# Two norms of a fused transformer pair: sums of squares taken behind each tile, the factor formed per token, the last division and the output split

## The reference, cut to what matters

```python
def rmsnorm_2(x, g):
    xf = x.astype(jnp.float32)
    y = xf * lax.rsqrt(jnp.mean(xf * xf, axis=-1, keepdims=True) + EPS)
    return (y * g.astype(jnp.float32)).astype(x.dtype)
...
        x = x + merged @ w_out[l]
        hn = rmsnorm_2(x, ffn_norm_g[l])
        gu = hn @ w_up[l]                     # 1024 -> 2 x 2816
        h = jax.nn.silu(gu[..., :FFN_HIDDEN]) * gu[..., FFN_HIDDEN:]
        x = x + h @ w_down[l]                 # 2816 -> 1024
    return rmsnorm_2(x, final_norm_g)
```

## Time and profile before

| what | value |
|---|---|
| time, median of 3 runs | 1966.1 us (1965.91 to 1969.23) |
| the profiled execution's own time | 1966.58 us |
| its span, first to last instruction | 1964.8 us |
| PE busy | 1749.0 us, 89% of the span |
| DVE / ACT / POOL busy | 441.5 / 282.9 / 116.6 us |
| chain that ended last | PE 76%, DMA 15%, SPq 3%, DVE 3%, ACT 2%, issue 1% |

### The profile page before, as it was taken

How to read it: one execution, slowest core, us unless ns; L and a number is a source line. 1 busy time by engine, 2 the same in 40 slices (tenths; PEclk the granted TensorE clock), 3 DMA queues, 4 the chain that set the end, 5 groups by cost and what they waited for, 6 DMA issues and landing times.

```text
span 1964.8 us, 20803 instructions
## 1 busy us (share of the span) xinstructions
PE 1749.0 (89%) x8422; PEld 1049.9 (53%) x8422; DVE 441.5 (22%) x1012; ACT 282.9 (14%) x570; POOL 116.6 (6%) x258
## 2 busy tenths in 40 slices
PE   6999999598998798969689779799998999899997
PEld 3534674153343234414234324387776788688885
DVE  2135221011111121202111111133555622111101
ACT  4024321011011010101001001023232210100001
POOL 1000000000000000004561000000020000000000
PEclk9999999898998898969899989899998999999998
DMA  9325357999999999999999999952443324434340
GB/s 379 111 88 214 115 203 318 420 413 415 417 417 407 419 413 414 398 420 417 415 417 417 422 418 415 404 182 86 161 147 116 129 83 174 149 129 172 129 150 22
DMA packets 135846, 547.02 MB, mean 278 GB/s; under 512 B 10109, under 2 KB 23549, under 8 KB 99774
## 3 DMA queue, kind: packets, MB, share of 16 engines
q1 hardware_dynamic: 129200, 529.83, 68.0%
q0 software_dynamic: 3200, 11.01, 1.5%
q10 hardware_dynamic: 3342, 4.77, 0.7%
HBM read 537.97 MB, written 7.60 MB: 278 GB/s over the span
## 4 chain that ended last, share of the span: by engine, by line
PE 76%; DMA 15%; SPq 3%; DVE 3%; ACT 2%; issue 1%; ACTq 0%; DVEq 0%
PE PS L1131 17%; PE PS L1157 8%; DMA ring<-in_w 7%; DMA arena<-in_w 6%; PE PS L2158 4%; PE PS L2168 4%; PE PS L2160 4%; PE PS L2002 4%; PE PS L2023 3%; SPq L1629 3%; PE PS L1168 3%; PE PS L1107 3%; PE PS L2015 3%; PE PS L497 2%; PE PS L1141 2%; PE PS L582 1%
## 5 line engine op out<-in xcount | busy, mean ns | idle before, releaser
L1131 PE MATMUL PS<-ring,arena 128*32 128x512 f32 (+2 forms) x1288 | 333.6, 680 | 67.9 <-DMA ring<-in_w 36.5
L1131 PE MATMUL PS<-arena 128*32 128x512 f32 (+2 forms) x760 | 217.7, 677 | 25.7 <-DMA ring<-in_w 19.7
L1131 PEld LDWEIGHTS PS<-ring,arena 128*32 128x32 f32 (+2 forms) x1288 | 102.6, 143 | 242.9 <-issue 242.8
L1157 PE MATMUL PS<-ring,arena 128*32 128x512 f32 (+2 forms) x584 | 147.1, 720 | 23.9 <-DMA ring<-in_w 19.3
L1157 PE MATMUL PS<-arena 128*32 128x512 f32 (+2 forms) x440 | 129.4, 679 | 28.8 <-DMA ring<-in_w 20.1
L1428 DVE TENSOR_SCALAR arena<-PS 128x512 f32<-128x512 f32 x28 | 19.2, 686 | 542.2 <-PE PS L1141 542.2
L1131 PEld LDWEIGHTS PS<-arena 128*32 128x32 f32 (+2 forms) x760 | 64.7, 143 | 120.8 <-issue 120.7
L1157 PEld LDWEIGHTS PS<-ring,arena 128*32 128x32 f32 (+2 forms) x584 | 43.7, 146 | 100.6 <-issue 99.6
L1157 PEld LDWEIGHTS PS<-arena 128*32 128x32 f32 (+2 forms) x440 | 41.4, 147 | 99.2 <-issue 99.2
L2158 PE MATMUL PS<-arena,ring 128*128 128x256 f32 x352 | 81.6, 386 | 6.3 <-DVE arena L2297 6.3
L2002 PE MATMUL PS<-arena,ring 128*128 128x256 f32 x384 | 86.1, 384 | 0.0
(11 more groups left out here) (433 smaller groups left out, 2043.1 us busy)
## 6 DMA issues: line engine op xcount, KB each, us to landing
ring<-in_w SPq DMA_DIRECT2D x234, 1024.0 KB, 18.4
arena<-in_w SPq DMA_DIRECT2D x150, 1024.0 KB, 19.3
ring<-in_w_ada SPq DMA_DIRECT2D x24, 1024.0 KB, 7.4
ring<-in_w_in SPq DMA_DIRECT2D x22, 1024.0 KB, 13.6
ring<-in_w_up SPq DMA_DIRECT2D x20, 1024.0 KB, 9.5
ring<-in_w_gate SPq DMA_DIRECT2D x16, 1024.0 KB, 6.1
ring<-in_w_down SPq DMA_DIRECT2D x11, 1024.0 KB, 7.3
ring<-in_w_out SPq DMA_DIRECT2D x8, 1024.0 KB, 5.1
```

The costliest lines, as they stand in the source:

```text
L1131: m = pe.matmul(bank(("up", i, b))[rows[n], :], xs[:, k, rows[n]], tiles[n][:, b * 512:(b + 1) * 512], start=k == 0, stop=False, skip_grou ...
L1157: m = pe.matmul(bank(("down", i, c))[rows[n], :], actT[:, k, rows[n]], tiles[n][:, a:a + 512], start=k == 0, stop=k == 7, skip_group_check ...
```

## The change

In the diff, `act`, `dve`, `pe`, `pool` and `sp` are the engines' own lists.

- **Middle norm, sums.** x2 tile f is squared by ScalarE as soon as it is added, into one of four buffers, and one x2 tile later TensorE multiplies the squares with one column of ones (`x2_sum`). ScalarE also writes `hw` = x * gain. The sum of tile 7 is put between the 7th and the 8th call of ff 0.
- **Middle norm, factor.** Root and reciprocal are taken of 128x2 numbers; two diagonal matrices and two calls with ones spread them ("x2factor") after ff 0. The products ff 0 and ff 1 use `hw` and are multiplied by the factor afterwards (`fft`); from ff 2 on the products use `hn` = hw * factor.
- **Weights.** The first two loads of `w_up` go into the two oldest of the six slots, the next two into 6 and 7, which now wait for x2 tile 0 and no longer for tile 7.
- **End.** Each "acc" bank is added to xv when it is finished. ScalarE squares two tiles at a time, VectorE adds the two squares (`add_pair`), TensorE takes four sums of pairs, then the factor as in the middle. VectorE finishes tiles 0 to 4; ScalarE has multiplied tiles 5 to 7 by the gain, and GpSimd multiplies them by the factor. The output leaves in four DMAs of 256 KB.
- The first Sqrt of each norm is called early on a constant (`eps.to_broadcast`).

```diff
-        sqf = [take(512) for _ in range(2)]
+        sqf = [take(512) for _ in range(4)]
         rff = take(256)
-        hn = take(8, 256)
+        hw, hn = take(8, 256), take(8, 256)
+        fft, ffd, ff_r = [take(512) for _ in range(2)], [take(128) for _ in range(2)], [sm(2) for _ in range(2)]
...
-        POST += [("x2", f) for f in range(8)]
+        POST += [("x2", 0)]
+        for f in range(1, 8):
+            POST += [("x2", f), ("x2sum", f - 1)]
...
         base = plan.turn % 6
-        plan.slots = [6, 7] + plan.slots[base:] + plan.slots[:base]
+        oldest = plan.slots[base:] + plan.slots[:base]
+        plan.slots = oldest[0:2] + [6, 7] + oldest[2:]
         plan.turn = 0
         for i in (6, 7):
-            plan.spent_at[i] = G["x2", 7].n
+            plan.spent_at[i] = G["x2", 0].n
         plan.rotate(range(8))
-        norm_plan("ffn2")
+        plan.group(("x2norm",), 7)
...
+            if f == 0:
+                plan.group(("x2factor",), 6)
...
-        norm_plan("fin2")
+        for i in range(4):
+            G["acc", i].n = plan.n + i
+        plan.n += 3
+        plan.group(("outnorm",))
+        plan.group(("outfactor",))
...
+            def x2_sum(f):
+                if f == 0:
+                    room(G["x2norm",])
+                w.wait_ge(x2_square, f + 1)
+                for t in range(2):
+                    i = pe.matmul(psum(("x2norm",), t, t + 1), sqf[f % 4][:, t * 128:(t + 1) * 128], ones[:, 0:1], start=f == 0 and t == 0, stop=f == 7, skip_group_check=True)
+                i.then_inc(pe_done, 1)
...
-            norm_sums("ffn2", sqf)
-            w.wait_ge(norm_done, 8)
+            def up(f, k, half):
+                src, key = (hw if f < 2 else hn), ("wg2", "wu2")[half]
+                if f == 0:
+                    w.wait_ge(hw_ready, k + 1)
+                elif f == 2:
+                    w.wait_ge(hn_ready, k + 1)
+                a = f % 4 * 128
+                return pe.matmul(psum(("ff", f), half * 256, half * 256 + 256), tile((key, f // 4), k, a, a + 128), src[:, k, :], start=k == 0, stop=k == 7, skip_group_check=True)
             for f in range(22):
-                s = ("ff", f)
-                room(G[s])
-                a = f % 4 * 128
+                room(G["ff", f])
                 for k in range(8):
-                    pe.matmul(psum(s, 0, 256), tile(("wg2", f // 4), k, a, a + 128), hn[:, k, :], start=k == 0, stop=k == 7, skip_group_check=True)
+                    if f == 0 and k == 7:
+                        x2_sum(7)
+                    up(f, k, 0)
                 for k in range(8):
-                    i = pe.matmul(psum(s, 256, 512), tile(("wu2", f // 4), k, a, a + 128), hn[:, k, :], start=k == 0, stop=k == 7, skip_group_check=True)
+                    i = up(f, k, 1)
                 i.then_inc(pe_done, 1)
+                if f == 0:
+                    w.wait_ge(ff_root, 4)
+                    room(G["x2factor",])
+                    for t in range(2):
+                        i = pe.matmul(psum(("x2factor",), t * 128, (t + 1) * 128), ones, ffd[t], start=True, stop=True, skip_group_check=True)
+                    i.then_inc(pe_done, 1)
             for n in range(4):
...
-                    w.wait_ge(moved[G["ff", k].bank], G["ff", k].use)
+                    if k < 2:
+                        w.wait_ge(ff_h, k + 1)
+                    else:
...
+                        if k == 21 and j % 2:
+                            i.then_inc(pe_done, 1)
+                if c < 10:
+                    i.then_inc(pe_done, 1)
+            room(G["outnorm",])
+            for i in range(4):
+                w.wait_ge(out_pair, i + 1)
+                for t in range(2):
+                    last = pe.matmul(psum(("outnorm",), t, t + 1), sqf[i][:, t * 128:t * 128 + 128], ones[:, 0:1], start=i == 0 and t == 0, stop=i == 3, skip_group_check=True)
+            last.then_inc(pe_done, 1)
+            w.wait_ge(ff_root, 8)
+            room(G["outfactor",])
+            for t in range(2):
+                i = pe.matmul(psum(("outfactor",), t * 128, (t + 1) * 128), ones, ffd[t], start=True, stop=True, skip_group_check=True)
+            i.then_inc(pe_done, 1)
...
-            norm_squares("ffn2", sqf, rff)
+                elif kind == "x2":
+                    f = s[1]
+                    if f == 0:
+                        act.activation(ff_r[0], eps.to_broadcast([128, 2]), ACT.Sqrt).then_inc(post_root, 1)
+                    w.wait_ge(moved[g.bank], g.use)
+                    if f >= 4:
+                        w.wait_ge(pe_done, plan.parts["x2sum", f - 4])
+                    act.activation(sqf[f % 4][:, 0:256], xv[:, f, :], ACT.Square).then_inc(x2_square, 1)
+                    act.activation(hw[:, f, :], xv[:, f, :], ACT.Copy, scale=Pm("ffn2_w", f)).then_inc(hw_ready, 1)
+            g = G["x2norm",]
+            w.wait_ge(pe_done, g.n)
+            act.activation(ff_r[0], psum(("x2norm",), 0, 2), ACT.Sqrt, scale=1.0 / 1024, bias=eps).then_inc(moved[g.bank], 1)
+            g = G["x2factor",]
+            w.wait_ge(pe_done, g.n)
+            act.activation(rff, psum(("x2factor",), 0, 256), ACT.Copy).then_inc(moved[g.bank], 1)
             for f in range(22):
                 g = G["ff", f]
-                w.wait_ge(pe_done, g.n)
-                if f >= 3:
-                    w.wait_ge(moved[G["ff", f - 3].bank], G["ff", f - 3].use)
-                act.activation(gsf[f % 3], psum(("ff", f), 0, 256), ACT.Sigmoid).then_inc(ff_s, 1)
+                if f < 2:
+                    w.wait_ge(moved[g.bank], g.use)
+                    act.activation(gsf[f], fft[f][:, 0:256], ACT.Sigmoid).then_inc(ff_s, 1)
+                else:
+                    w.wait_ge(pe_done, g.n)
+                    if f in (3, 4):
+                        w.wait_ge(ff_h, f - 2)
+                    elif f > 4:
+                        w.wait_ge(moved[G["ff", f - 3].bank], G["ff", f - 3].use)
+                    act.activation(gsf[f % 3], psum(("ff", f), 0, 256), ACT.Sigmoid).then_inc(ff_s, 1)
+            act.activation(ff_r[1], eps.to_broadcast([128, 2]), ACT.Sqrt).then_inc(post_root, 1)
             for i in range(4):
                 w.wait_ge(moved[G["acc", i].bank], G["acc", i].use)
-            w.wait_ge(norm_done, 8)
-            norm_squares("fin2", sqf, rff)
+                act.activation(sqf[i].rearrange("p (a b) -> p a b", a=2), xv[:, 2 * i:2 * i + 2, :], ACT.Square).then_inc(out_square, 1)
+                for k in range(max(2 * i, 5), 2 * i + 2):
+                    w.wait_ge(out_square, i + 1)
+                    act.activation(xv[:, k, :], xv[:, k, :], ACT.Copy, scale=Pm("fin2_w", k)).then_inc(out_scaled, 1)
+            g = G["outnorm",]
+            w.wait_ge(pe_done, g.n)
+            act.activation(ff_r[1], psum(("outnorm",), 0, 2), ACT.Sqrt, scale=1.0 / 1024, bias=eps).then_inc(moved[g.bank], 1)
+            g = G["outfactor",]
+            w.wait_ge(pe_done, g.n)
+            act.activation(rff, psum(("outfactor",), 0, 256), ACT.Copy).then_inc(moved[g.bank], 1)
...
+            def factor(n, key):
+                g = G[key]
+                w.wait_ge(moved[g.bank], g.use)
+                w.wait_ge(post_root, n + 1)
+                dve.reciprocal(ff_r[n], ff_r[n]).then_inc(ff_root, 1)
+                w.wait_ge(ff_root, 4 * n + 1)
+                if n:
+                    w.wait_ge(pe_done, G["x2factor",].n)
+                dve.tensor_scalar(ffd[0], ident, ff_r[n][:, 0:1], None, ALU.mult).then_inc(ff_root, 1)
+                dve.tensor_scalar(ffd[1], ident, ff_r[n][:, 1:2], None, ALU.mult).then_inc(ff_root, 2)
+            def add_pair(i):
+                w.wait_ge(out_square, i + 1)
+                dve.tensor_tensor(sqf[i][:, 0:256], sqf[i][:, 0:256], sqf[i][:, 256:512], ALU.add).then_inc(out_pair, 1)
+            factor(0, ("x2norm",))
             for f in range(22):
                 key = ("ff", f)
                 g, sg = G[key], gsf[f % 3]
-                w.wait_ge(ff_s, f + 1)
-                own.count(dve.tensor_tensor(sg, psum(key, 0, 256), sg, ALU.mult))
-                own.wait()
-                dve.tensor_tensor(hh[:, f, :], psum(key, 256, 512), sg, ALU.mult).then_inc(moved[g.bank], 1)
-            w.wait_ge(pe_done, G["wd", 10])
+                if f < 2:
+                    one = G["x2factor",]
+                    w.wait_ge(moved[one.bank], one.use)
+                    w.wait_ge(pe_done, g.n)
+                    dve.tensor_tensor(fft[f].rearrange("p (a b) -> p a b", a=2), psum(key).rearrange("p (a b) -> p a b", a=2), rff.unsqueeze(1).to_broadcast([128, 2, 256]), ALU.mult).then_inc(moved[g.bank], 1)
+                    if f == 0:
+                        w.wait_ge(hw_ready, 8)
+                        for k in range(8):
+                            dve.tensor_tensor(hn[:, k, :], hw[:, k, :], rff, ALU.mult).then_inc(hn_ready, 1)
+                    w.wait_ge(moved[g.bank], g.use)
```

(32 more changed lines are left out.)

17 lines of the change are left out of this document (10 added, 7 removed).

## The result

The changed kernel takes 1951.5 us (median of 8 runs, 1948.2 to 1958.7), the kernel before 1968.1 (8 runs, 1964.1 to 1969.7). The ratio is 0.9923, with a 95% interval from 0.9907 to 0.9939. That is 12.0 to 18.3 us less; 17.9 were forecast, and the time lies inside the range. The profiled execution has a span of 1950.7 us against 1964.8.

The account below looks back on a forecast made before the run. TensorE held 76% of the span; the chain left it for a 12.10 us gap before ff and a 21.06 us end. Gains of 9.5 (middle) and 8.4 (end), 17.9 in all, gave 1948.2 us against 1966.1; range 1945.0 to 1953.5.

Parts of the forecast that it names:

- The gap and the clock: Between x2 and ff: 12.10 us without a weight product, then 16 records at half clock taking 5.67, not 3.45; 14.3 us available.
- Both steps: Between x2 and ff 0: removing the 12.10 us gap, and running ff 0's first 16 records in 3.45 us, not 5.67.
- The sums: Middle norm, behind the x2 tiles: eight small sums at 0.53 us each give back 4.2 us; bounds 3.4 and 7.6.
- The rival in which sums don't overlap: Middle norm: small sums cost 0.95 us each, so the middle gains only 5.7 and the kernel takes 1952.0; chance 12%.
- Covers: Middle norm: tile 7's sum waits for nothing; `hn` is done 13.0 us after x2, first read at 15.5, 2.5 cover.
- The loads: First `w_up` loads, in the new slot order, all arrive before ff needs them: priced at nothing; still late, 6.0 us lost.
- The end: From the last w_down product to the span's end: 12.7 us instead of 21.06, 8.4 less; bounds 10.9 and 15.1.
- The half clock in the spread: Last norm: the factor's spread finds the granted clock at 0.50, adding 0.7 us to 0.95 at full clock.
- The contention: Final multiplications: VectorE and GpSimd, two SBUF inputs each, slow each other; last tile ready at 9.5 us, not 8.0.
- The rival in which each transfer pays its time alone: Output DMAs: each pays 2.9 us in turn, end 19.0 us, gain 11.6, kernel 1954.5; chance 8%.
- The slower rival: In x2: small sums starve the clock, seven tiles at 0.50 cost 24.2 us, kernel 1972.4; chance 3%.
- the one with the end at its lower bounds: Last norm and output: bursts keep the clock up and the two engines don't disturb each other, kernel 1946.4; chance 10%.

## Why the prediction was right

**The gap and the clock.** Both steps held: 14.3 us were to be had, ff 0 starts behind x2 at full clock.

**The sums.** 8 x 0.53 = 4.2 was forecast from another tile's rows; measured 0.34 + 0.11 = 0.45 each, 3.6 in all. The row of 0.42 there began behind small calls of another kind. The spread cost 0.44, without the 0.11 for a change of shape that I had put on it. So the middle gained 10.3, not 9.5. The rival in which sums don't overlap (1952.0) is refuted by the kernel that takes them twice.

**Covers.** The last sum waited for nothing; `hn` was done 12.1 us after x2, forecast 13.0, wanted at 15.1.

**The loads.** Priced at nothing with the new slots and at 6 us without: nothing and 7.6. The step was right; the price of its absence had the stall in the wrong place and left out the clock behind it.

**The end.** 12.7 was forecast and 12.8 measured, which is closer than its terms were. Pair 3 ended 2.1 us after the last product (forecast 2.4), the multiplications began at 5.6 (6.2), the last tile was ready at 9.1 (9.5), the last DMA was issued near 9.7 (9.5). The half clock in the spread was there, at 0.5 and not 0.7; at full clock the spread takes 0.72 and not 0.95. That it was there is in part luck: in two of ten traces it was not, and the end is then 12.3. The contention was there too, but otherwise shared out: I took 0.6 for a tile on VectorE and 1.1 on GpSimd, and it was 0.69 and 0.81. Sized from 512-element instructions, the last tile came out nearly right and the parts did not. Without contention the last tile would by the same rows be ready at 6.2 + 3 x 0.73 = 8.4, not at the 8.0 that I wrote; the 12.7 doesn't use it. I also missed that three DMA issues queue on SP behind VectorE's late tiles; the last transfer, at 2.7 and not 2.9, hid a part of it. The rival in which each transfer pays its time alone (19.0) is refuted by the 12.8 itself.

**What the change is for.** I took the token factor as part of the gain and did not ask what the old form would do in the new places. The runs say that it costs 0.6 in the middle. At the end it costs 0.3 with the spread at the clock of 0.50 and gains 0.2 with it at 1.00.

**The slower rival** (small sums pull the clock down in x2) did not come: 1.00 all through x2 and ff. Nor did the one with the end at its lower bounds: the lower clock and the contention were both there.

## What to carry to other kernels

A norm between two products costs what stands between the last tile and the first product, so take the sums behind the tiles, let the first products run on unscaled input, and ask of each part of such a change what it does alone: in the middle here the place of the sums, the products that run ahead and the order of the weight slots made the gain, and the more elaborate form of the factor took a little of it back. Before a stall is removed, look at what was loaded under it; the stall of 12.1 us hid loads worth 7.6. When work is shared between VectorE and GpSimd, count the SBUF inputs of both: with the factor in SBUF, handing three tiles over made the end 1.3 us longer than VectorE alone, and with VectorE's factor in PSUM it came out 0.1 shorter. And before a difference of half a microsecond at the end of a kernel is put down to an edit, look at the granted clock in both traces.

## What the runs showed of the hardware

- VectorE and GpSimd with two SBUF inputs each: 128x256 takes VectorE 0.69 on average (five in 3.46; the first 0.94 on the chain) and GpSimd 0.81; with one of VectorE's inputs in PSUM, 0.41 and 0.69.
- With the same instructions, the granted clock in the end's spread was 0.50 in eight traces and 1.00 in two, and in the trace with added products it fell though TensorE had been busy without a gap in the 2 us before; four records of 128 columns take 1.24 or 0.72, four of one column 0.85 to 0.93 or 0.61.
- A DMA of 256 KB lands in 2.2 us when the issues on its queue are 0.8 apart, and the last one in 2.7 when three issues come within 1 us; an issue takes SP 0.4 to 0.5.
- A product of one column with a fresh 128x128 weight takes 0.11 us in a row of its kind, and a group of them costs its big neighbours 0.11 once, whether it has four records or eight; four records of 128 columns in the stream (0.44) and two of 256 (0.43) cost theirs nothing that the trace shows.
